# Retention with zero-padded keys and state, an earlier first head of stick attention, and two smaller edits, in a two-block transformer kernel

## What is computed

```python
def retention(q, k, v):                       # 4 heads, dk 64, dv 128, chunks of 128 tokens
    q = rotary(q); k = rotary(k) * (dk ** -0.5)
    scores = jnp.einsum('bhnid,bhnjd->bhnij', qc, kc) * decay[None, :, None]
    o_intra = jnp.einsum('bhnij,bhnje->bhnie', scores, vc)
    chunk_kv = jnp.einsum('bhnjd,hj,bhnje->nbhde', kc, k_decay, vc)
    ... # state = state * g_chunk + kv, from chunk to chunk
    o_inter = jnp.einsum('bhnid,hi,nbhde->bhnie', qc, q_decay, r_prev)
    return o_intra + o_inter

def stick_breaking(q, k, v):                  # 8 heads of 64
    z = (q @ k.T) * scale                     # causal, strict
    w = jnp.exp(log_sigmoid(z) + suffix_sum(log_sigmoid(-z)))
    return w @ v

def hgrn2(q, f_logit, i, lb):                 # 4 heads of 128, gated linear attention
    decay = jnp.exp(jnp.where(tril, b[t] - b[s], -jnp.inf))   # b: cumulative log gate
    attn = jnp.einsum('bhtk,bhtsk,bhsk->bhts', qc, decay, kc)
```

## Time and profile before

| what | us |
| --- | --- |
| median of 3 runs | 2588.99 (2585.32 to 2596.64) |
| the profiled execution | 2613.81 |
| its span, first to last instruction | 2612.0 |
| PE busy, share of the span | 2218.1, 85% |
| DVE, ACT, POOL busy | 1290.0, 1029.8, 584.1 |
| mean granted TensorE clock | 0.909 |

### The profile page before, as it was taken

How to read it: one execution, slowest core, us unless ns; L and a number is a source line. 1 busy time by engine, 2 the same in 40 slices (tenths; PEclk the granted TensorE clock), 3 DMA queues, 4 the chain that set the end, 5 groups by cost and what they waited for, 6 DMA issues and landing times. The chain is left out here.

```text
span 2612.0 us, 34392 instructions
## 1 busy us (share of the span) xinstructions
PE 2218.1 (85%) x12244; PEld 1825.9 (70%) x12244; DVE 1290.0 (49%) x2211; ACT 1029.8 (39%) x1828; POOL 584.1 (22%) x672
## 2 busy tenths in 40 slices
PE   7996997999797599999289997968859799956768
PEld 5885887999685466675278885758748687845657
DVE  3333665555543666665451210357755343417843
ACT  3333654555431255554231210046543233327632
POOL 1003101522010122231110001446522000027822
PEclk9997998999898699999699998579989899987879
DMA  4787776321344399995652312243163424141152
GB/s 152 215 239 198 221 219 165 98 64 40 118 146 171 126 359 370 355 342 209 217 206 97 113 49 77 61 87 73 37 219 108 153 95 148 69 135 47 42 184 90
DMA packets 216721, 399.15 MB, mean 153 GB/s; under 512 B 90513, under 2 KB 111377, under 8 KB 203905
## 3 DMA queue, kind: packets, MB, share of 16 engines
q1 hardware_dynamic: 177008, 314.52, 38.0%
q10 hardware_dynamic: 28384, 61.62, 6.2%
q0 software_dynamic: 11184, 21.13, 2.2%
HBM read 300.16 MB, written 114.85 MB: 159 GB/s over the span
## 5 line engine op out<-in xcount | busy, mean ns | idle before, releaser
L78 PE MATMUL pe_acc<-pe_w,hT 128*128 128x512 f32 x960 | 222.3, 393 | 0.0
L78 PEld LDWEIGHTS pe_acc<-pe_w,hT 128*128 128x128 f32 x960 | 181.7, 190 | 37.8
L78 PE MATMUL ex_gu<-hT,ex_xT 128*128 128x512 f32 x792 | 194.2, 401 | 0.8 <-DVE hT L2349 0.8
L2349 DVE TENSOR_TENSOR hT<-ex_raw,hT 128x2048 fp32r<-128x2048 f32 x66 | 150.9, 2288 | 87.1 <-ACT hT L2320 87.1
L78 PE MATMUL pg_acc<-hT,pg_w 128*128 128x512 f32 x768 | 180.0, 396 | 8.9 <-DVE pg_w L257 8.9
L78 PEld LDWEIGHTS pg_acc<-hT,pg_w 128*128 128x128 f32 x768 | 145.5, 190 | 42.4 <-DVE pg_w L257 9.3
L78 PEld LDWEIGHTS ex_gu<-hT,ex_xT 128*128 128x128 f32 x792 | 147.4, 189 | 34.5 <-DVE hT L2349 1.2
L2320 ACT ACTIVATE hT<-ex_raw 128x2048 fp32r<-128x2048 f32 x66 | 126.2, 1913 | 41.4 <-PEq L47 23.9
L296 DVE COPY pe_o<-pe_acc 128x512 f32<-128x512 f32 x28 | 19.3, 690 | 206.7 <-PE pe_acc L78 206.7
L1725 PE MATMUL ab_op<-ab_v,ab_pT 128*128 128x64 f32 x1024 | 121.3, 272 | 0.0
L2278 PE MATMUL ex_dn<-ex_wd,ex_hT 128*128 128x512 f32 x264 | 118.7, 592 | 0.8 <-ACT ex_hT L2314 0.8
(11 more groups left out here) (473 smaller groups left out, 4990.9 us busy)
## 6 DMA issues: line engine op xcount, KB each, us to landing
ex_raw<-in_w_gate SPq DMA_DIRECT2D x33, 1024.0 KB, 7.2
ex_raw<-in_w_up SPq DMA_DIRECT2D x33, 1024.0 KB, 11.1
ex_wd<-in_w_down SPq DMA_DIRECT2D x33, 1024.0 KB, 14.2
pe_raw<-in_even_w_in SPq DMA_DIRECT2D x6, 2048.0 KB, 9.1
pg_raw<-in_odd_w_in SPq DMA_DIRECT2D x5, 2048.0 KB, 9.4
scr_q<-pa_o SPq DMA_DIRECT2D x32, 256.0 KB, 3.8
scr_k<-pa_o SPq DMA_DIRECT2D x32, 256.0 KB, 3.8
hT<-scr_k SPq DMA_DIRECT2D x16, 512.0 KB, 6.8
```

The lines of the kernel that those rows point to most:

```text
L78: mm = pe.matmul(out, a(p, k), b(q, k), start=(k == 0 and i == 0), stop=(k == n - 1 and i == 2))
L2349: dve.tensor_tensor(split(s, LO)[:, :, g, :], raw[:, s % NW, g, :].rearrange("p (k n) -> p k n", k=8), split(s, HI)[:, :, g, :].bitcast(F3 ...
```

## The change

1. Joined norms: PE multiplies tile 0 before turn 1, which goes between its 18th and 19th matmul. ACT and DVE split tile 0 as soon as the weights are split. In `Rows.load` the gain row is loaded behind tile 0 instead of ahead of it.
2. Experts: the loop has 7 turns with two bodies each.
3. Retention: keys lie in `re_kz`, one plane of 128 partitions a head with zeros in the other head's half, and so does the state; all products have 128 rows. DVE computes the odd half of the rotation and POOL the even half. ACT copies the transposes out. x of chunk 0 is loaded first. SP, ACT and POOL also load and split head 0 of stick attention, into parts of hT, which is free there.
4. Stick attention starts with masks, values and head 1; its split buffers are the parts of hT.
5. hgrn2: one difference of 512 elements a level; ACT takes the exponential in two halves with scale -1 and 1; for unit 0 DVE multiplies the keys.

```diff
 # project, PE
+                def first_steps(k):
+                    pe.wait_ge(lo_ok, k + 1)
+                    if r and k == nk - 2:
+                        r.pe_turn(pe, 1)
...
-                            for t in range(j + 1 if j else 0, min(j + 2, NT)):
+                            for t in range(j + 1 if j else 0, min(j + 2, NT) if j else 1):
...
 # project, ACT and DVE (lx is 1 in the even projection, 0 in the first)
+                        elif lx and s == 2:
+                            r.act_turn(act, 0)
...
+                            r.dve_turn(dve, 0)
...
 # experts, further
-            with eng.Fori(1, NOV) as j:
-                with eng.If(n > j):
-                    body(j)
+            with eng.Fori(0, (NOV - 1) // 2) as r:
+                with eng.If(n > r * 2 + 1):
+                    for i in range(2):
+                        body(r * 2 + (i + 1))
...
 # retention, PE
-                            mm = pe.matmul(o, qkT[p0:p0 + 64, u, 4 + j, :], state[p0:p0 + 64, u, j, :], start=False, stop=True)
+                            mm = pe.matmul(o, qkT[:, u, 2 + j, :], state[:, u, h, :], start=False, stop=True)
...
-                            mm = pe.matmul(sps[h % 2][:, j * P:(j + 1) * P], qkT[p0:p0 + 64, u, 2 + j, :], qkT[p0:p0 + 64, u, j, :],
-                                           start=True, stop=True)
+                            mm = pe.matmul(sps[h % 2][:, j * P:(j + 1) * P], kz[:, u, h, :], qkT[:, u, j, :], start=True, stop=True)
...
 # retention, ACT
+                def turn_back(s):
+                    u = s % 2
+                    act.wait_ge(turned, s + 1)
...
+                    act.activation(qkT[:, u, 0:2, :].rearrange("p j n -> p (j n)"), tp[0][:, 0:2 * P], ACT.Copy).then_inc(T_ok, 1)
+                    for b in range(2):
+                        r = slice(64 * b, 64 * b + 64)
+                        act.activation(kz[r, u, :, :].rearrange("p (j b) n -> p j b n", b=2)[:, :, b, :],
+                                       tp[0][r, 2 * P:4 * P].rearrange("p (j n) -> p j n", j=2), ACT.Copy).then_inc(T_ok, 1)
+                    act.activation(qkT[:, u, 2:4, :].rearrange("p j n -> p (j n)"), tp[1][:, 0:2 * P], ACT.Copy).then_inc(T_ok, 1)
...
 # hgrn2, DVE and ACT
-                        dve.tensor_tensor(dv[:, :, 0, :], mid, bv[:, :, 0, :], ALU.subtract).then_inc(df_ok, 1)
-                        dve.tensor_tensor(dv[:, :, 1, :], bv[:, :, 1, :], mid, ALU.subtract).then_inc(df_ok, 1)
+                        dve.tensor_tensor(whole(df[:, g % 2, :], m), whole(b[:, :], m), mid, ALU.subtract).then_inc(df_ok, 1)
+                        if n == 0 and l:
+                            keys_first(l - 1)
...
-                        act.activation(ex[:, g % 2, :], df[:, g % 2, :], ACT.Exp).then_inc(ex_ok, 1)
+                        for half, sign in enumerate((-1.0, 1.0)):
+                            act.activation(ev[:, :, half, :], dv[:, :, half, :], ACT.Exp, scale=sign).then_inc(ex_ok, 1)
```

More of the change, by code:

```diff
@@ L222, in _ @@
                             pe.wait_ge(copied[u], uses[g][j])
-                        before = (lambda k: pe.wait_ge(lo_ok, k + 1)) if g == 0 and j == 0 else None
+                        before = first_steps if g == 0 and j == 0 else None
                         if ch["kind"] == "row":
@@ L321, in _ @@
                             split_hi(act, 0)
+                            if not lx:
+                                r.act_turn(act, 0)
                         if s >= lx + 4:
@@ L500, in load @@
         u = t % self.ns
-        if t == 0 and self.post is not None:
-            sp.dma_start(self.prow[:, :], self.post.partition_broadcast(P)).then_inc(self.post_in, 16)
         if t == 0 and self.z_gain is not None:
@@ L520, in load @@
                 sp.dma_start(self.e[c][:, u, :], rows(self.expert_rows[0], c * NT + t)).then_inc(self.tile_in[u], 16)
+        if t == 0 and self.post is not None:
+            sp.dma_start(self.prow[:, :], self.post.partition_broadcast(P)).then_inc(self.post_in, 16)
     def pool_begin(self, pool):
@@ L2405, with stick_parts, retention @@
 RH, RDV = 4, 128
-def retention(nc, ident, rows_in, C, out):
+def stick_parts(hT):
+    store = hT[:, :, :, :].rearrange("p a k s -> p (a k s)")
+    return [store[:, 2 * n * S:(2 * n + 2) * S].rearrange("p (u s) -> p u s", u=2) for n in range(3)]
+def retention(nc, ident, rows_in, C, out, next_qk, lead):
     QK = 2 * RH
@@ L2428, in retention @@
         gch = st.sb("re_gch", [P, 2])
-        qkT = st.sb("re_qkT", [P, 2, 6, P])
+        qkT = st.sb("re_qkT", [P, 2, 4, P])
+        kz = st.sb("re_kz", [P, 2, RH, P])
         sc = st.sb("re_sc", [P, 2, RH * P])
-        state = st.sb("re_state", [P, 2, 2, RDV])
+        state = st.sb("re_state", [P, 2, RH, RDV])
+        zeros_ok = st.sem("re_zeros_ok")
         ob = st.sb("re_ob", [P, 2, RH * RDV])
+        lead_q, lead_k = (st.sb("re_lead_" + n, [P, S]) for n in "qk")
+        qs, kh, kl = lead
+        lead_in, lead_hi, lead_lo = (st.sem("re_lead" + n) for n in ("_in", "_hi", "_lo"))
         tp = [st.ps(f"re_tp{i}", [P, BANK]) for i in range(2)]
@@ L2449, in _ @@
                 sp.dma_start(gch[:, :], C["ret_gchunk"]).then_inc(consts_in, 16)
-                for t in range(NT):
+                for t in range(1, NT):
                     if t >= 4:
@@ new lines, in rotate @@
+            def rotate(eng, t, products, step, op, c0, a, b):
+                u = t % 2
+                eng.wait_ge(x_in[t % 4], 16 * (t // 4 + 1))
+                if t >= 4:
+                    eng.wait_ge(turned, t - 3)
+                    eng.wait_ge(decayed, t - 3)
+                xv = x[:, t % 4, 0:512].rearrange("p (h d) -> p h d", d=64)
+                c = cs[:, t, 0:32].unsqueeze(1).to_broadcast([P, QK, 32])
+                s = cs[:, t, 32:64].unsqueeze(1).to_broadcast([P, QK, 32])
+                even, odd = xv[:, :, 0:32], xv[:, :, 32:64]
+                first, second = ((even, c), (odd, s)) if c0 == 0 else ((even, s), (odd, c))
+                eng.tensor_tensor(a[:, u, :, :], first[0], first[1], ALU.mult).then_inc(products, 1)
+                eng.tensor_tensor(b[:, u, :, :], second[0], second[1], ALU.mult).then_inc(products, 1)
+                eng.wait_ge(products, 2 * (t + 1))
+                eng.tensor_tensor(rot[:, t % 4, :, c0:c0 + 32], a[:, u, :, :], b[:, u, :, :], op).then_inc(step, 1)
@@ L2551, in _ @@
                         dve.wait_ge(kv_ok, t + 1)
-                        dve.wait_ge(state_ok, 2 * t + 1)
+                        dve.wait_ge(state_ok, RH * t + 1)
                         if t >= 1:
                             dve.wait_ge(o_ok, t)
-                        for j in range(2):
-                            dve.scalar_tensor_tensor(out=state[:, 1 - u, j, :], in0=state[:, u, j, :], scalar=gch[:, j:j + 1],
-                                                     in1=kv[:, j * RDV:(j + 1) * RDV], op0=ALU.mult, op1=ALU.add).then_inc(state_ok, 1)
+                        for h in range(RH):
+                            r, j = slice(64 * (h % 2), 64 * (h % 2) + 64), h // 2
+                            dve.scalar_tensor_tensor(out=state[r, 1 - u, h, :], in0=state[r, u, h, :], scalar=gch[r, j:j + 1],
+                                                     in1=kv[r, j * RDV:(j + 1) * RDV], op0=ALU.mult, op1=ALU.add).then_inc(state_ok, 1)
                     if s < NT:
@@ L2592, in stick_breaking @@
         qraw, kraw = (st.sb("sb_" + n, [P, 2, S]) for n in ("qraw", "kraw"))
-        qs, kh, kl = (st.sb("sb_" + n, [P, 2, S], F32R) for n in ("qs", "kh", "kl"))
+        qs, kh, kl = lead
         v = st.sb("sb_v", [P, 2, NT, DV])
@@ L2861, in split, with whole, pool_products @@
             return x.rearrange("p (n h m) -> p n h m", h=2, m=m)
+        def whole(x, m):
+            return x.rearrange("p (n m) -> p n m", m=2 * m)
+        def pool_products(g):
+            return g if g <= NL else 2 * g - NL
         def of_unit(buf, n):
@@ L3017, in prep @@
                         g, m = n * NL + l, LEVELS[l]
-                        pool.wait_ge(ex_ok, g + 1)
+                        pool.wait_ge(ex_ok, 2 * (g + 1))
                         for half, src in enumerate((kk[:, n % 4, :], of_unit(q, n))):
+                            if n == 0 and half == 0:
+                                continue
                             pool.tensor_tensor(split(qk[:, n % 3, l, :], m)[:, :, half, :], split(src, m)[:, :, half, :],
@@ L3382, in second @@
 def second(nc, A, C, scr, ident, hT, out):
-    retention(nc, ident, scr["erows"], C, scr["ret"])
-    stick_breaking(nc, ident, 8, scr["sqkT"], scr["srows"], C, scr["stick"])
+    retention(nc, ident, scr["erows"], C, scr["ret"], scr["sqkT"], stick_parts(hT))
+    stick_breaking(nc, ident, 8, scr["sqkT"], scr["srows"], C, scr["stick"], stick_parts(hT))
     mix_out(nc, "em", ident, hT, A["even_w_out_2"][0], None,
```

129 lines of the change are left out of this document (77 added, 52 removed).

## The result

| | median us | executions | ratio to before |
| --- | --- | --- | --- |
| before, same chip | 2590.68 | 4 (2585.32 to 2596.64) | |
| the change | 2571.97 | 4 (2570.36 to 2574.20) | 0.9926 (0.9905 to 0.9947) |
| profiled execution of before / of the change | 2613.81 / 2571.34 | | |

The account below looks back on a forecast made before the run. PE, busy 85% of the span, was taken as the bound, slow or idle in the changed stretches. Terms -32 - 8.5 - 3.2 + 0.8 + 0 - 2.5 = -45.4, taken off the median 2589.0, gave 2544 us; range 2528 to 2568.

Parts of the forecast that it names:

- Retention, steady part: Retention chunks: padding removes row switches, the clock rises early, 9.17 us chunks become 4.7; with the start, -32 us.
- the last step of the sum: Whole kernel: -45.4 us on the profiled 2613.8 gives 2568.4, scaled by 0.9905 to the median runs: 2544 us.
- The chunk of 4.7: Retention at full clock: PE needs 4.2 us a chunk, the load loop 4.6; 4.7 us taken.
- The rival on the collision: Retention: DVE's rotation and decay run 1.8 times as long beside POOL, chunk 5.5 us, total 2550; chance 10%.
- Start of the retention: Retention's beginning: x issued first and fewer POOL instructions bring chunk 0's outputs 4.8 us earlier.
- Stick attention's start: Stick attention: first matmul waits for masks alone, 3.0 us after the first load for 12.2; -8.5 us.
- Experts' loop: POOL's empty loop behind the experts: seven turns fewer, -3.2 us, or nothing if its drain waits for a fixed time.
- First projection: Joined norms there: product 0 starts earlier, but turn 2 waits for tile 1's split; +0.8 us.
- hgrn2: hgrn2: seven of POOL's 14 products before unit 0 go to DVE, -2.5 us; later units 0.
- The clock stays low: Retention: padding removes switches but the clock mostly stays 0.50; gain there 11 us, total 2565; chance 19%.
- The switch is not of rows: Retention outputs: the 0.30 us comes from changing operands or accumulating, so padding does not remove it; 2577; chance 3%.
- The exponential's halves: hgrn2 on ACT: halves charged by the run; slower from 0.81 us more a level, 2599 at 1 us; chance 2%.

Follow-up runs that it names:

- e13: The kernel before, unchanged, run for one more profile; 2595.51 us.
- e15: The kernel before, unchanged, run for a further profile; 2581.80 us.
- e5: The change, unchanged, run again for its spread; 2565.27 us median, ratio to before 0.9893.
- e3: The kernel before with all of the change but its retention and stick attention; 2588.94 us median, ratio 0.9973.
- e11: The change, unchanged, run again as a partner on the same chip; 2569.66 us median, ratio to before 0.9902.
- e4: The change with the state's output products on 64 rows again, scores still padded; 2576.08 us median, ratio to before 0.9928.
- e7: The change with both state outputs and scores on 64 rows again; 2585.61 us median, ratio to before 0.9970.
- e9: The change with the scores on 64 rows in pairs again, state outputs still padded; 2570.84 us median, ratio to before 0.9905.
- e2: The kernel before with only the retention and stick attention of the change; 2574.49 us median, ratio 0.9928.
- e6: The change with eight buffers for x in the retention instead of four; 2564.03 us median, ratio to before 0.9884.
- e10: The change with PE's idle gaps around retention and ahead of stick attention filled by unused products; 2570.95 us median, ratio to before 0.9905.
- e12: The change with PE's idle gaps filled by unused products and eight buffers for x; 2565.0 us median, ratio to before 0.9881.
- e1: The kernel before, unchanged, 12 executions; 2593.28 us median, ratio 0.999, profiled execution 2608.2 us.
- e16: The kernel before with 24 unused products in PE's idle time at the start of the retention; 2588.73 us median, ratio 0.9981.

## Why the prediction was wrong, step by step

- **Retention, steady part, and the last step of the sum (the failed ones).** The working took the 9.17 us chunk at clock 0.50 as what the kernel before does. It is what one execution of it did. In typical ones the clock rises at chunk 0 or 1 and the old chunk is 5.2 us (e13 to e15). B is 39.5 to 43.4 us there, where the sum set out from 63.1. The new form came near its forecast: its seven steps take 34.5 to 38.0 us (33.9 forecast). So padding gains only the 0.2 us an output at the full clock, and the load loop takes that back. -32 became about -6.1 (A -3.6, B -2.5 between the means of e13 to e15 and of the three profiles of the change); in the first pair of profiled executions it was -26.4. Scaling by 0.9905 did not repair that: it took the 25 us between the profiled execution and the median as spread evenly over the program, while 20 to 24 us of it lay in this one stage. The warning was in the numbers of before: a profiled execution 17 us above the slowest of the three runs shown.
- **The chunk of 4.7.** Too short by a little: the four middle steps take 5.3 to 7.4 us, the load loop (forecast at 4.6). DVE's three rotation instructions take 2.2 us there and not 1.1 (0.94 us for a product beside POOL's, 0.41 alone), so the collision was larger than the 0.5 us allowed for it. The rival on the collision, with chunks of 5.5, was nearer: in e5, where the clock doesn't dip, the four take 5.3 to 6.2. The last two steps take 4.1 and 3.8.
- **Start of the retention**: -3.6 for -4.8. The rotation starts 4.6 to 4.9 us behind the issue of x (4.2 forecast), and by the profile the constant `re_cs`, which was taken to be in time, releases it; POOL's three instructions take 2.7 us beside DVE for 2.15. **Stick attention's start**: 3.1 us from first load to first product, 3.0 forecast; C is 9 us shorter, -8.5 forecast. Right. D stayed within its scatter (175.9 to 181.0 against 175.8 to 180.7), so nothing shows head 1 late.
- **Experts' loop**: -3.2 forecast, -4.1 measured: POOL's drain starts 10.2 us behind the experts' last product for 14.3. It still takes 5.46, so it is no wait for something at a fixed time. **Even projection**: 0 forecast. The span between the last products of the experts and of the even projection is 371.6 in the mean of the change, e3, e5 and e11 and 376.0 in that of five profiles of before, -4.4 with the loop's -4.1 in it. Its first product comes 41.1 us behind the experts' last for 54.5, and next to nothing of these 13 us reaches its end.
- **First projection**: the order and the 1.08 us wait came as forecast, and +0.8 may be right: the last product lies at 211.0 to 214.6 us, mean 213.4, in seven profiles with the old order, at 212.5 to 216.4, mean 214.1, in eleven with the new. The scatter is larger than the difference, so it stays open.
- **hgrn2**: -2.5 forecast for the fill, -1.9 measured (31.4 to 29.5 us from the odd projection's last product). But the products of all units, whose later ones were taken to gain and lose nothing, take 130.1 to 131.0 us for 129.4 to 129.5, 0.6 to 1.5 more. The pair of halves at 0.72 us for 0.63 goes the same way; that it is the cause is not shown. Net about -0.7.
- **The rivals.** "The clock stays low" pointed at the right resource and the wrong kernel: the clock is up in the new form, but it mostly was in the old one too. "The switch is not of rows" is out by e4. The exponential's halves cost 0.09 us a level, far from the 0.81 at which the whole gain would go. The rule of the Trainium skill that I weighed ("TensorE: Matmul & The Clock Gate", "Why this matters for your kernels") would have made the padding a loss. The runs disagree: without it the retention is 10 us longer (e7 against e5, B). Pairing the scores alone, as the rule advises, neither gained nor lost (e9).
- **A bound.** The -36 given for chunks of 4.2 comes out at -35 by the prediction's own terms; nothing rests on it.

With typical terms the sum is -6.1 -9 -4.4 -0.7, about -20, against 18.7, 28 and 26 us by medians in three comparisons. The rest, up to 8 us, may come from executions in which the clock rises late in the old form; that was not separated.

## To carry to other kernels

Before a gain is taken from a profiled execution, hold its time against the spread of the runs: where it lies outside, some stage in it was not typical, and a stretch at a low granted clock is the first suspect. Work out the gain of such a stretch at both clocks, and let the forecast follow the clock that the median run has; the mean clock of each run tells which that is. Look at the longest executions too: a form that gains little at the full clock may still be worth having where the old one is at times caught at the low one. Of the 49 executions with padded outputs (the change, e2, e6, e9, e10, e12) none was over 2583 us.

## What was not expected of the hardware

- PE can be busy throughout and stay at granted clock 0.50 for long: 48.4 us in before, 36.8 in e1 (1639.0 to 1675.8). With the same code in the same place the clock is up 20.5 us after its fall in another execution (e13). Ten of the 95 executions of before, the profiled one among them, were at 2607 us or more.
- Fillers raised the clock 5.4 us (e16) and 5.7 us (e10) after they began; in e16 they ended at 1629.8, and the clock was down at 1633.8. There PE was idle for 4 us in between, and the next work ran at the low clock. In e10 the gap was 1 us and the clock stayed up until 1627.5, yet nothing was gained.
